# An expert-mixing kernel on one core: which of two gathers in a pair is issued first

## What is computed

```python
def peer_block(xb, w_q, sub_keys, expert_u, expert_v):
    q = (xb @ w_q).reshape(T, PEER_HEADS, 2, PEER_HALF)
    s = jnp.einsum('thpd,hpkd->thpk', q, sub_keys)
    sv, si = lax.top_k(s, PEER_TOPK)
    ...
    top_s, pos = lax.top_k(cand, PEER_TOPK)
    eidx = jnp.take_along_axis(cidx, pos, axis=-1)
    gate = jax.nn.softmax(top_s.astype(jnp.float32), axis=-1).astype(xb.dtype)
    u = jnp.take(expert_u, eidx, axis=0)
    act = jax.nn.gelu(jnp.einsum('thkd,td->thk', u, xb))
    v = jnp.take(expert_v, eidx, axis=0)
    return jnp.einsum('thk,thkd->td', gate * act, v)
```

## Time and profile before

| | us |
|---|---|
| median of three runs | 4076.16 |
| the profiled execution | 4073.35 |
| its span | 4071.4 |
| GpSimd busy | 2056.6 (51%) |
| VectorE busy | 2019.2 (50%) |
| TensorE busy (matmul) | 2006.1 (49%) |
| ScalarE busy | 685.6 (17%) |
| software gathers, time of their packets | 70.2% of 16 engines' span |

### The profile page before, as it was taken

The page is one execution under the profiler, slowest core; times in us unless marked ns, Lnnn a source line. Parts: engine busy times, 40 slices in busy tenths (PEclk is TensorE's granted clock), DMA queues, the critical chain, the costliest instruction groups (busy, mean ns, idle before and its releaser), DMA issues.

```text
span 4071.4 us, 34938 instructions
## 1 busy us (share of the span) xinstructions
PE 2006.1 (49%) x9949; PEld 931.6 (23%) x9949; DVE 2019.2 (50%) x4967; ACT 685.6 (17%) x1897; POOL 2056.6 (51%) x2098
## 2 busy tenths in 40 slices
PE   8998963443433333333437954333333333333447
PEld 3554541111111111111213431111111111111213
DVE  1425265555555555555552255555555555555551
ACT  2112121111111111112111111111111111112112
POOL 1413136565655555555562045555555555555661
PEclk9998886666666666666568976666666666666668
DMA  5312359898988888889997268888888888889992
GB/s 199 124 52 83 134 188 340 324 342 307 345 331 331 323 329 330 327 329 361 335 341 260 83 251 333 330 330 327 333 331 328 323 330 336 325 323 357 341 362 103
DMA packets 334241, 1168.56 MB, mean 287 GB/s; under 512 B 36026, under 2 KB 39380, under 8 KB 331732
## 3 DMA queue, kind: packets, MB, share of 16 engines
q0 software_dynamic: 294912, 1073.87, 70.2%
q1 hardware_dynamic: 39124, 92.27, 6.1%
HBM read 1163.92 MB, written 2.10 MB: 286 GB/s over the span
## 4 chain that ended last, share of the span: by engine, by line
another core or an unknown queue 47%; PE 18%; ACT 10%; issue 8%; DVE 6%; POOL 3%; DMA 3%; POOLq 0%; ACTq 0%; DVEq 0%
PE banks L701 14%; ACT ring L1405 4%; PE banks L1039 4%; DVE scr L1903 2%; ACT L1397 2%; ACT L1385 2%; POOL scr L646 2%; POOL ring L652 2%; DMA ring<-in_peer_up,idx_v 1%; DMA ring<-in_expert_v,idx_v 1%; ACT scr L1385 0%; ACT hT L1223 0%; ACT ring L1375 0%; ACT scr L1397 0%
## 5 line engine op out<-in xcount | busy, mean ns | idle before, releaser
L1039 PE MATMUL banks<-ring 128*32 128x512 f32 x4096 | 874.6, 950 | 1642.2 <-ACT ring L1405 736.6
L1903 DVE CUSTOM_DVE_ANT_0 scr<-scr,banks 128x1024 f32<-128x1024 f32 x1024 | 1207.2, 1218 | 578.7 <-DMA scr<-in_expert_u,idx 271.1
L646 POOL DMA_INDIRECT scr<-in_expert_u,idx x512 | 480.9, 939 | 542.4 <-DVE idx L1882 156.0
L646 POOL DMA_INDIRECT scr<-in_peer_down,idx x512 | 480.7, 939 | 422.9 <-DVE scr L1903 155.8
L1039 PEld LDWEIGHTS banks<-ring 128*32 128x32 f32 x4096 | 177.5, 153 | 2126.3 <-issue 1983.2
L652 POOL DMA_INDIRECT ring<-in_expert_v,idx_v x512 | 480.2, 938 | 312.7 <-issue 145.7
L652 POOL DMA_INDIRECT ring<-in_peer_up,idx_v x512 | 480.6, 939 | 306.5 <-issue 150.2
L701 PE MATMUL banks<-ring,scr 128*128 128x128 f32 (+1 forms) x2112 | 287.4, 297 | 8.6 <-ACT ring L1427 5.2
L701 PEld LDWEIGHTS banks<-ring,scr 128*128 128x128 f32 x2112 | 259.7, 201 | 85.0 <-issue 81.6
L1375 ACT ACTIVATE ring<-banks 128x256 f32<-128x256 f32 x64 | 24.5, 383 | 1457.6 <-remote 1391.4
L701 PE MATMUL banks<-ring,hT 128*128 128x512 f32 x512 | 224.6, 596 | 1.8 <-DVE hT L1808 1.0
(11 more groups left out here) (211 smaller groups left out, 2067.6 us busy)
## 6 DMA issues: line engine op xcount, KB each, us to landing
ring<-in_w_mod SPq DMA_DIRECT2D x12, 2048.0 KB, 8.8
ring<-in_w_in SPq DMA_DIRECT2D x7, 2048.0 KB, 12.9
scr<-in_peer_w_q SPq DMA_DIRECT2D x1, 8192.0 KB
scr<-in_peer_down,idx POOLq DMA_INDIRECT x512
ring<-in_peer_up,idx_v POOLq DMA_INDIRECT x512
scr<-in_w_q SPq DMA_DIRECT2D x1, 8192.0 KB
scr<-in_expert_u,idx POOLq DMA_INDIRECT x512
ring<-in_expert_v,idx_v POOLq DMA_INDIRECT x512
```

The costliest lines, as they stand in the source:

```text
L646: nc.gpsimd.indirect_dma_start(u_rows[:, k % SLOTS, :], None, table_u, bass.IndirectOffsetOnAxis(idx[:, h % IDX_SLOTS, k:k + 1], 0)).then_ ...
L1039: last = nc.tensor.matmul(psum[2 + c][32 * g:32 * g + 32, :], spread[:, h % 2, k, :], v_rows[k % SLOTS][:, c * CW:(c + 1) * CW], start=(h ...
L1903: V.tensor_tensor_reduce(u_rows[:, k % SLOTS, :], u_rows[:, k % SLOTS, :], xn, 1.0, 0.0, ALU.mult, ALU.add, dots[:, h % 2, k:k + 1]).then_ ...
```

## The change

In each pass over k the up gather of this head is issued first and the down gather of the next head second. Number, size, indices, buffers and waits of the gathers stay as they are; each wait still stands just before its own gather.

```diff
                         for k in range(TOPK):
+                            v_gather(first + h, h, k)
                             if u_too:
                                 u_gather(first + (h + 1), (h + 1) % PH, k)
-                            v_gather(first + h, h, k)
```

## The result

The changed kernel takes 4089.63 us (median of 17 runs, 4070.95 to 4104.71), the kernel before 4073.99 beside it (17 runs, 4065.28 to 4091.31). The ratio is 1.0041, with a 95% interval of 1.0026 to 1.0055: slower by 0.4%. The forecast was 4085. The profiled execution of after took 4096.99 us (span 4095.0), 23.6 more than that of before.

The account below looks back on a forecast made before the run. The prediction took GpSimd's gather issue plus two stalls a head as the bound, with TensorE's signals waiting for GpSimd's pauses. Terms +26 + 1 - 13 - 5 = +9 us on 4076.2 gave 4085 us; range 4056 to 4130.

Parts of the forecast that it names:

- (1): GpSimd's queue: 16 and 16 gathers between the two stalls instead of 17 and 15; 39.17 us before, 39.18 after, nothing.
- (2): Before the up gather of rank 0: same wait for the same TensorE product, 4.2 us as before, nothing.
- Stall B: GpSimd idle before the up gather of rank 0, until TensorE uses the previous head's rank 8; 4.2 us a head.
- late heads: Heads in which ScalarE's copy of the weights starts after GpSimd's pause before rank 8 has begun.
- (3): Before rank 8: the wait now ends with TensorE's use of rank 0, not a dot product; +26 us in 44 heads.
- Stall A: GpSimd idle before the down gather of rank 8, released by a VectorE dot product; 7.97 us on average.
- (4): 13 heads with weights before the pause: up gather passes at once, two gathers fewer left; -29 to -6, taken as -13 us.
- Early heads: Heads in which ScalarE's copy of the weights starts before GpSimd's pause before rank 8; 13 in the prediction.
- (5): Three heads at a stage's or block's start, dot product far behind TensorE: -7 to -4, taken as -5 us.
- (6): Last down gather comes 2.48 us nearer the pause before rank 0; VectorE's 2.98 us idle covers it, nothing charged.
- The faster rival: Before rank 8: weights' signal comes before the pause in more heads, up to -3.1 us each; 4039 with 15; chance 0.16.
- no change: Rival: the gathers' landing rate is the bound, one stall loses what the other gains; 4076 us, chance 0.14.

Follow-up runs that it names:

- experiment 1: Kernel before with the new order (up gather first) at rank 8 alone: 4108.25 us, ratio 1.007.
- experiment 2: Kernel before with the new order at all ranks but 8: 4074.57 us, ratio 0.9993.
- experiment 8: Half rows: kernel before with each gather fetching 2048 instead of 4096 bytes, leaving out half of the computation: 3419.11 us, ratio 0.9655, on chip B.
- experiment 12: The new order at rank 8 alone once more, against the kernel before, on chip E: 3536.41 us, ratio 0.9984.
- experiment 3: Kernel before with GpSimd waiting ahead of rank 4 until TensorE has rearranged the weights: 3934.13 us, ratio 0.9647.
- experiment 4: Kernel before with six memsets of an unused piece ahead of rank 4, some 4.6 us without a gather: 4049.21 us, ratio 0.9926.

## Why the prediction was right, and where it was not

The time (4085 for 4089.63) was right, the sign was the forecast's own, and the loss came for the reason given, on the chip where it was measured. By its size, over 0.3%, it falls to the side that had a chance of 0.41. The steps, by the table above:

- (1) *Gathers between stalls.* Right: 16 and 16.
- (2) *Stall B.* Right within 0.2 us: 3.37 and 3.38 us by the mean of late heads, 3.78 and 3.58 by their median. It had been given as 4.2 for all, a mean that holds other stalls too.
- (3) *Stall A ends with TensorE's product.* Right in mechanism: rank 8 alone carries the loss (experiments 1 and 2). Predicted +26 in 44 heads, 0.6 each; measured 0.68 in 45 heads, +31.
- (4) *Early heads.* -13 predicted, -15 measured, and that is luck. The step put the gain on the pause before rank 8, where it is 3.93 to 3.80 us, some 2 us in all. The 15 stand before rank 0 (4.65 to 3.47 us next to early heads), and they stand there in experiments 1 and 2 as well (195 and 187 us against 212), though in experiment 2 rank 8 has its old order. So the reasoning of this step did not give them; what did is open.
- (5) *Starts of stages.* -5 taken. The three heads meant have 6.7 less before rank 8, but one of them now stalls 3.6 before the next rank 0: 3.0 less. (The 5 less of the stages' first and last heads are mostly others.)
- (6) *Nothing lost of the cover.* Right: experiment 2.
- *Not in the sum:* the heads changed sides, five from early to late and three back, net two at +4.6 each, +9. The faster rival had them going the other way. And 6 us of longer gathers and 6 outside the stages, which I put down to chance. These make up the way from +9 to +23.6, of which the medians keep 15.6.

**What it did not see** is how far its base reached. "Why a signal waits for a pause no row tells; that it does is what the sum rests on": the sentence is right, and on chips B to E the base is not there. The same code there has no late signals, and the edit gains 0.4%. All 44 heads of step (3) fall away with it. What is left is the case that the rival *no change* described, gathers near the landing rate. The middles of the first and the second stage in the kernel before on chip D, columns as in experiment 8:

```profile
1100.00:1900.00 800.00, 361.14 (x2172) 154.86 (x2173) 516.37 (x1304) 151.15 (x465) 563.20 (x598) 0.66 1.01 398
2300.00:3300.00 1000.00, 454.27 (x2808) 196.30 (x2800) 657.94 (x1683) 185.79 (x572) 712.95 (x757) 0.67 1.02 402
```

and that of the first stage in the first profile of the kernel before:

```profile
1100.00:1900.00 800.00, 298.19 (x1822) 127.33 (x1823) 442.43 (x1113) 124.85 (x389) 472.02 (x503) 0.65 0.89 335
```

DMA engines that are busy throughout, at 398 and 402 GB/s, against 0.89 and 335. Even there the order was worth something. The wait at rank 8 went from a dot product to TensorE's product there too, but by experiment 12 that alone does not account for the gain. The Trainium skill, "DMA: Bandwidth & Descriptors", section Specifications, has about 358 GB/s as one core's share of HBM. The trace, of a kernel on one core, goes above it: 402 GB/s over 1000 us here, 410 in the earlier trace rows.

## What to carry to other kernels

Where an instruction starts long after the step that it waits for, and always the same time after another engine stops issuing, an early pause of that engine may be worth more than any order of the work: here an added wait of 2.5 us a head won 3.5%, on the one chip where signals were late. Then measure on more than one chip. An edit of 0.4% had either sign (1.0041 and 0.9956), the added wait that won 3.5% on one chip gave 1.0018 together with the new order on another, and a wait put two ranks earlier cost 9.4% there.

## What the runs showed of the hardware

**Signals were late in the first measurements and on chip A, and prompt on four other chips.** On chip A (4080 us), as in the first profiles, the signals of TensorE's rearranged weights and q products mostly come in a pause of GpSimd's indirect DMAs: the copy of the weights starts a median of 14.7 us after the rearrangement in the kernel before and 16.1 in the changed one, in 52 of 64 heads within a pause and about 3 us after its start. On B to E (3541 to 3543 us) it starts 0.20 us after. GpSimd's gathers take 0.94 us on all. Whether it is the chip or how it was set up at the time can't be told: the runs with late signals all came before those with prompt ones, and no chip was used twice at a distance; nor is it told which chip the first measurement had. What holds a signal back stays open too; half rows did not run on chip A.

**The delay is on TensorE's side, and a pause is not its whole rule.** The trace also has the times at which semaphores change. In the first profile the semaphore of the rearranged weights changes a median of 14.6 us after the end of TensorE's step and that of the q products 17.3, and ScalarE starts within about 0.1 us of it; ScalarE's own signals, as far as the trace has them, change 0.01 us after their instruction. As the profile models the ends of matmuls, the trace does not tell whether TensorE finishes late or signals late. The moved indices' semaphore is late too, by 5.3 us, yet in only 9 of 61 heads does it change in a pause; the scores' is prompt in four heads of five. So "TensorE's signals wait for a pause" holds for the two signals that the sum used, and not for all.

**Where signals are late, the trace itself has gaps.** Of VectorE's 1024 dot products' signals it holds 608 in the first profile, 596 in experiment 1 and 414 in experiment 3, and all of them in the profiles of chips B to E. Every timed run has its span from a trace, so no run shows the kernel untraced, and that tracing has a part in the late signals is a rival that nothing here rules out.

**TensorE itself can start its instructions one at a time on chip A.** In experiment 4, some q products:

```profile
2718.85 0.27 PE L706 MATMUL banks<-ring,scr 128*128 128x128 f32 x1 [2.52 <-issue]
2721.65 0.37 PE L706 MATMUL banks<-ring,scr 128*128 128x128 f32 x1 [2.53 <-issue]
2723.78 0.37 PE L706 MATMUL banks<-ring,scr 128*128 128x128 f32 x1 [1.76 <-issue]
2725.88 0.37 PE L706 MATMUL banks<-ring,scr 128*128 128x128 f32 x1 [1.73 <-issue]
```

They wait for nothing that the profile shows, and start 2.1 to 2.8 us apart. Idle times of 1.3 to 3 us of this kind stand before 182 of TensorE's records in the two stages there and before 146 in experiment 3, but before 28 in the first profile and 7 in that of the changed kernel, and before none or one on chips B to E.
